# Prompt attention: the next tile's queries one pair of heads earlier, the gates one pair later

## What is computed

```python
q_b = (rmsnorm(cq, g_q) @ w_uq).reshape(B, T, H_B, D_NOPE + D_ROPE)          # 8 heads of 64 + 32
q_b = jnp.concatenate([q_b[..., :D_NOPE], rope(q_b[..., D_NOPE:], pos)], axis=-1)
...
s = jnp.einsum('bqhd,bkhd->bhqk', qb, k, preferred_element_type=F32) * scale
mask = k_chunk[None, :] <= (pb // CHUNK)[:, None]                            # CHUNK = 64
p = jax.nn.softmax(jnp.where(mask[None, None], s, -jnp.inf), axis=-1)
o_b = jnp.einsum('bhqk,bkhd->bqhd', p.astype(v.dtype), v)
...
o_b = o_b.reshape(B, T, W_B) * jax.nn.silu(z_b)
```

## Time and profile before

| | |
|---|---|
| median of 3 runs | 4291.05 us (4288.51 to 4294.73) |
| the profiled execution | 4292.63 us |
| its span in the trace | 4290.9 us |
| prompt's attention in it, first scores to last gating | 1578 to 2262 us |
| TensorE busy over the span | 3981.1 us (93%) |
| VectorE / ScalarE busy over the span | 1808.3 us / 1356.3 us |

### The profile page before, as it was taken

One profiled execution on the slowest core, in us unless ns is written; L12 is line 12 of the kernel. 1 busy time (PEld: TensorE's weight loads), 2 busy tenths in 40 slices (PEclk: granted clock), 3 DMA queues, 4 the chain that ended last, 5 costly groups with the idle time before them and its releaser, 6 DMA issues. The chain is left out here.

```text
span 4290.9 us, 59679 instructions
## 1 busy us (share of the span) xinstructions
PE 3981.1 (93%) x23109; PEld 2783.1 (65%) x23109; DVE 1808.3 (42%) x4545; ACT 1356.3 (32%) x3492; POOL 162.7 (4%) x188
## 2 busy tenths in 40 slices
PE   7899999969999788999998879899999999979999
PEld 1677777748999535666663434477777777667776
DVE  0333433435555335555553322222212112189996
ACT  0111111125555226555551300022222111145553
POOL 1000000010110000000000000000000000000000
PEclk9899999979999889999999889899999999989999
DMA  9111111151110100000001062311111111143343
GB/s 365 38 59 41 41 62 41 40 91 52 60 53 21 49 30 29 22 15 15 8 8 35 16 237 103 115 69 59 68 54 68 64 69 69 78 158 146 131 154 106
DMA packets 112768, 315.64 MB, mean 74 GB/s; under 512 B 34644, under 2 KB 50840, under 8 KB 106328
## 3 DMA queue, kind: packets, MB, share of 16 engines
q1 hardware_dynamic: 109832, 287.38, 19.1%
q0 software_dynamic: 2768, 25.96, 1.7%
HBM read 203.57 MB, written 109.73 MB: 73 GB/s over the span
## 5 line engine op out<-in xcount | busy, mean ns | idle before, releaser
L1861 PE MATMUL e_p<-e_hT,w_ahead 128*128 128x128 f32 x3264 | 410.6, 276 | 5.6 <-DMA e_w<-w_in_o 5.6
L1861 PEld LDWEIGHTS e_p<-e_hT,w_ahead 128*128 128x128 f32 x3264 | 389.2, 193 | 13.6 <-issue 13.6
L465 PE MATMUL a_p<-w_even,a_hT 128*128 128x512 f32 (+2 forms) x1088 | 391.8, 521 | 0.0
L453 PEld LDWEIGHTS a_p<-a_hT,w_even 128*128 128x128 f32 x3264 | 367.5, 193 | 26.5 <-ACT a_z L438 19.7
L453 PE MATMUL a_p<-a_hT,w_even 128*128 128x128 f32 x3264 | 370.6, 276 | 12.9 <-ACT a_z L438 11.3
L465 PEld LDWEIGHTS a_p<-w_even,a_hT 128*128 128x128 f32 x1088 | 205.4, 190 | 174.1 <-issue 122.0
L1406 PE MATMUL q_sps<-kT,q_qT 96*128 96x512 f32 (+3 forms) x640 | 267.9, 550 | 20.2 <-ACT q_qT L1485 18.5
L1565 DVE TENSOR_REDUCE q_mx<-q_sps 128x1 f32<-128x512 f32 (+4 forms) x320 | 181.5, 583 | 247.6 <-PE q_sps L1406 246.7
L1727 PE MATMUL c_b<-c_w,c_oc 128*128 128x512 f32 x544 | 240.3, 603 | 20.4 <-DMA c_w<-w_out_e 9.2
L2234 PE MATMUL h_b<-h_w,h_oT 128*128 128x512 f32 x544 | 250.4, 595 | 0.0
L1820 ACT ACTIVATE e_r<-e_p 128x512 f32<-128x512 f32 x68 | 40.6, 597 | 525.2 <-PE e_p L1867 304.0
(11 more groups left out here) (398 smaller groups left out, 6355.6 us busy)
## 6 DMA issues: line engine op xcount, KB each, us to landing
scr_qkg<-e_r SPq DMA_DIRECT2D x68, 512.0 KB, 2.6
h_rq<-scr_qkg SPq DMA_DIRECT2D x17, 2048.0 KB, 10.5
wa<-w_ada SPq DMA_DIRECT2D x16, 1536.0 KB, 12.4
scr_iz<-e_r SPq DMA_DIRECT2D x34, 512.0 KB, 2.6
scr_qkv<-a_cv SPq DMA_DIRECT2D x17, 768.0 KB, 3.2
d_sc<-scr_qkv SPq DMA_DIRECT2D x17, 768.0 KB, 4.4
w_even<-w_in_e POOLq DMA_DIRECT2D x8, 1620.0 KB, 35.1
w_ahead<-w_in_o POOLq DMA_DIRECT2D x6, 2048.0 KB, 18.9
```

Of the source, the lines that this page charges most:

```text
L453: mm = pe.matmul(bank[g][:, (c % 4) * P:(c % 4 + 1) * P], w[:, k, c * P:(c + 1) * P], hT[:, p, k, :], start=k == 0, stop=k == KD - 1)
L465: mm = pe.matmul(dst[:, 0:b - a], hT[:, p, k, :], w[:, k, a:b], start=k == 0, stop=k == KD - 1)
L1861: mm = pe.matmul(bank[n % 4][:, c * P:(c + 1) * P], w[k][:, a:a + P], hT[:, p, k, :], start=k == 0, stop=k == KD - 1)
```

## The change

For every tile that has a next one, `queries(m+1)` moves from pair 2 to pair 1 and `queries_T(m+1)` from pair 3 to pair 2, on TensorE and on ScalarE. VectorE's `rotate(m+1)` moves from the head of pair 3 to the end of pair 1. For every tile that has a preceding one, `gates_T(m-1)` and `gated(m-1)` move from pair 1 to pair 2; on TensorE `gates_T` stands ahead of `queries_T` there. The waits in `transposes` move with them. `latents` and `gates` stay. No instruction is added or removed, and the lists of SP and POOL are the same.

```diff
--- before.py
+++ after.py
@@ -1412,11 +1412,11 @@
                 if n:
                     pe.wait_ge((pt_a, pt_b)[p], n)
                 pe.wait_ge(exp_r, z.exps(2 * j + p, b))
-                if b == 0 and p == 0 and j == 1 and z.m:
+                if b == 0 and p == 0 and j == 2 and z.m:
                     pe.wait_ge(obT_r, z.m)
+                if b == 0 and p == 1 and j == 1 and after(z):
+                    pe.wait_ge(qb_out, 2 * z.m + 3)
                 if b == 0 and p == 1 and j == 2 and after(z):
-                    pe.wait_ge(qb_out, 2 * z.m + 3)
-                if b == 0 and p == 1 and j == 3 and after(z):
                     pe.wait_ge(qT_out, z.m + 2)
                 for i in range(4 * b, min(4 * b + 4, z.kt)):
                     mm = pe.transpose(tps[p][:, i % 4 * P:(i % 4 + 1) * P], Pr[:, slot(z, 2 * j + p), i * P:(i + 1) * P], ident[:, :])
@@ -1441,11 +1441,11 @@
                 nz, nj = following(z, j)
                 if j == 0 and after(z):
                     latents(z.m + 1)
-                if j == 1 and z.m:
+                if j == 2 and z.m:
                     gates_T(z.m - 1)
+                if j == 1 and after(z):
+                    queries(z.m + 1)
                 if j == 2 and after(z):
-                    queries(z.m + 1)
-                if j == 3 and after(z):
                     queries_T(z.m + 1)
                 if nz:
                     scores(nz, 2 * nj)
@@ -1595,10 +1595,8 @@
 
             def pair(z, j):
                 nz, nj = following(z, j)
-                if j == 1 and z.m:
+                if j == 2 and z.m:
                     gated(sizes[z.m - 1])
-                if j == 3 and after(z):
-                    rotate(z.m + 1)
                 if nz:
                     maxima(nz, 2 * nj)
                 for b in range(z.ng):
@@ -1607,6 +1605,8 @@
                         maxima(nz, 2 * nj + 1)
                 if j == 0 and z.m:
                     gates(sizes[z.m - 1])
+                if j == 1 and after(z):
+                    rotate(z.m + 1)
 
             rotate(0)
             maxima(sizes[0], 0)
```

## The result

The changed kernel takes 4256.6 us in the median of 4 runs (4249.19 to 4258.07), the kernel before beside it 4289.8 (4286.37 to 4294.73): a ratio of 0.9918, with a 95% interval from 0.9906 to 0.9931. The forecast was 4255 in a range from 4244 to 4268.

A forecast was written before the change was run, and what follows sets the result against it. The prediction took TensorE, busy 93% of the span, to bound the kernel. Waits gave 37.6 - 4.7 - 2.0 - 1.1 = 29.8, say 30 us, the clock 6: 4291 - 36 = 4255 us, range 4244 to 4268.

The forecast's parts named there:

- The waits that go: TensorE's waits for copies (19.8 us), rotation (10.2), factors (6.6) and gating (1.0) go: 37.6 us together.
- What stays of the rotation's wait: Ahead of the queries' turning, now in pair 2: gates' turning covers 0.50 us a tile, 4.7 us stay.
- What stays of the copies' wait: Ahead of pair 2's transposes: scores and first transposes cover too little in tiles 0 to 2; 2.0 us stay.
- The gating: VectorE's gating, 0.69 us long, in its new place in pair 2: nothing of it shows on TensorE.
- New late comers: TensorE newly waits for exponentials in tiles 7 and 11 and for probabilities in tiles 0 and 1: 1.1 us.
- The clock: Slow stretches at pair 3's breaks in tiles 1, 2 and 8 go: 7.6 us by count, 6 taken.
- two rules: Whether long gaps alone lower TensorE's clock (sum 30 us) or frequent short breaks do too (38 to 40).
- The sum: Whole kernel: 30 us from waits plus 6 from the clock, 36 us off 4291, giving 4255.
- Rival (c): TensorE meets ScalarE's late exponentials at heads of pairs 2 and 3: some 15 us given back, 4276; chance 0.06.

The follow-up runs named there:

- gates_only: Kernel before with only the gates' turning and the gating moved from pair 1 to pair 2; 4276.9 us against 4286.3, ratio 0.9973.
- turn_late: Changed kernel with only the turning of the queries put back in pair 3; 4267.6 us, ratio 0.9954 to the kernel before.
- fill: Kernel before plus needless identity turnings at pair 3: 9 behind the queries' turning, 8 ahead in tiles 0 to 3; 4279.8 us, ratio 0.9981.
- the second set of runs: Changed kernel, unchanged, timed again beside the kernel before; 4251.5 us against 4285.9, ratio 0.9921.
- rotate_mid: Changed kernel with the rotation in the middle of pair 1 instead of at its end; 4255.9 us, ratio 0.9928 to the kernel before.
- mid0: Changed kernel with the second head's scores always behind the first group's transposes; 4265.5 us, ratio 0.9954 to the kernel before.
- fill_gates: Kernel before plus needless identity turnings ahead of the gates' turning in pair 1 of tiles 1 to 4; 4284.4 us, ratio 0.9997.

## Why the prediction was right

*The waits that go.* Forecast: 37.6 us, with 0.16 us for each restart. Between the two traces TensorE's idle times in the stage fell from 48.2 us (46.2 and the start's 2.0) to 23.1, 25.1 less. The breaks in that view became fewer by 26, 61 for 87: 34 went (15 for the copies, 9 for the rotation, 8 for the factors and 2 for the gating) and 8 came (3 for the copies ahead of transposes, 5 told below). At 0.16 us that is another 4.2. It makes 29.3 us, against a forecast of 29.8 for what goes less what stays. The other way round, 35.6 us less 25.1 and the clock's 6.4 leaves 4.1 for the 26 breaks, 0.16 each. Waits of 0.9 us that the slow stretches had covered stand in both terms; without them it is 3.2 us, 0.12 each. The parts don't bear this out one by one: in gates_only the same count leaves 2.1 us (12.5 - 3.1 - 6.4 - 0.9) for 2 breaks fewer. So the restarts are worth 3 to 4 us of the whole, and 0.16 for each isn't shown.

*What stays of the rotation's wait.* Forecast 4.7, measured 2.9 and 4 restarts, 3.6. It stays in tiles 0 to 3 (1.30, 0.62, 0.53, 0.50); the 0.33, 0.11, 0.32 and 0.11 forecast for tiles 4, 5, 8 and 9 don't show. The cover was taken too small: in tiles 1 to 3 the idle time fell by 0.58 to 0.59 us, not by the 0.50 to the next start. That leaves 0.08 us of the 0.67 and 0.66 of tiles 4 and 8.

*What stays of the copies' wait.* Forecast 2.0 in tiles 0 to 2, measured 0.91, 0.59 and 0.27 with three restarts, 2.3. These are rows of TensorE in the changed kernel's tile 0:

```profile
1596.94 0.64 PE L1380 MATMUL q_sps<-k_ident,q_qb 128*96 128x128 f32 x4 [1.30 <-DVE q_qb L1557]
1597.42 0.60 PE L1380 MATMUL q_t<-k_ident,q_qb 128*96 128x128 f32 x4
1597.85 0.39 PE L1406 MATMUL q_sps<-kT,q_qT 96*128 96x128 f32 x2
1598.08 0.27 PE L1422 MATMUL q_t<-k_ident,q_P 128*128 128x128 f32 x1
1599.27 0.44 PE L1422 MATMUL q_t<-k_ident,q_P 128*128 128x128 f32 x1 [0.91 <-ACT q_qT L1485]
```

Scores and one transpose pair stand between turning and wait, as the cover was counted.

*The gating.* Nothing of it shows, as forecast; turn_late shows what it costs (2.1 us) where the queries' turning doesn't cover it.

*New late comers.* Forecast 1.1. One shows as a row, 0.69 us ahead of the scores of tile 12, which wait for the last exponentials of tile 11; in tile 7 there was no new one. In tiles 1 and 2 three more breaks stand ahead of the products (8 for 5, 2.1 us for 1.4), and there is one more of 0.24 us for copied probabilities. gates_only, which moves no queries, has more of both too (11, 3.5 us, and 32), so they are not the moved queries' doing.

*The clock.* Forecast 6 us, from three stretches that go. All three went. They had cost 6.4 us by the same instructions at either clock, 35.6 - 29.3 leaves 6.3, and fill's price gives 5.9. The prediction's count, half of the slow time, would have been 7.6. It came out less because at the higher clock waits show that the slow one had covered, 0.9 us: in the three stretches measured under fill, gates_only waits 0.43, 0.27 and 0.24 us where the kernel before doesn't. The forecast took 6 and not 7.6 for another reason, breaks that stay in pair 2 of tiles 0 to 2, so its closeness is in part luck. The cause was right only in part. That filling pair 3's breaks holds the clock is shown in tile 0. That a break of that length brings a slow stretch is not so, as gates_only shows, so it was partly luck that the changed kernel had none behind tile 0.

The prediction weighed two rules. The one on long gaps alone, "HAM oscillation — how this bites in real kernels" in the Trainium skill, "TensorE: Matmul & The Clock Gate", doesn't fit this case: in the kernel before no break of TensorE between the stage's first scores and its end is longer than 1.3 us, and four slow stretches stand behind such breaks.

*The sum.* 36 us were forecast; the stage gave 35.6, the profiled span 34.6, the medians 33.2 and, in the second set of runs, 34.4. Rival (c), ScalarE next in line, was worth little here, but it is what stopped rotate_mid and mid0.

## What to carry to other kernels

When the engine that bounds the kernel stands in a fixed spot until another engine has copied its result away, move the step that needs the copy one unit of independent work earlier, and check both what covers it now and what it covered before: here the gates' turning shortens the rotation's wait and the queries' turning hides the gating. Count a break as its idle row plus the overlap that is lost at the restart. And price the clock by itself before crediting it to an edit: by the time that one and the same stretch of instructions takes in two traces at either clock, or by filling the breaks with work that does nothing. A run with filled breaks can also shift all that follows, so compare the clock at the first place that isn't shifted.

## What the runs showed of the hardware

A break costs TensorE more than its idle row: rows of 0.66 us have their successor start after 0.50, an overlap of 0.16 that a break loses, and over the whole change 3.2 to 4.1 us were left for 26 breaks, 0.12 to 0.16 each. And work that does nothing can pay: with 9 to 17 needless transposes a tile the kernel was 6 us faster, and TensorE kept 2.4 GHz behind the stage's first 11 us. At 1.2 GHz the same six scores took 4.63 us instead of 2.42, but slow stretches of 3 to 7 us cost 1.4 to 2.9 us. The stretches at 1.2 GHz behind tile 0 stood at the same places of the stage in three traces (two of the kernel before, one of fill_gates), tile 8's to within 0.4 us, and were gone in all traces of the kernels with one or both parts of the change, also where the breaks of pair 3 had been left.
